# Order of the expert pieces and form of the bias products in a hybrid layer's expert stage

## The chip, the cores and the metric

The kernel runs on one core of a Trainium2 chip. The metric is the device time of one execution in microseconds; lower is better. A profile of one execution shows what each engine did: TensorE (PE, its weight loads apart as PEld), VectorE (DVE), ScalarE (ACT), GpSimd (POOL) and SyncE (SP), which here issues most of the DMAs.

## What is computed

One decoder layer on 1024 tokens of width 1024: attention and convolution, then a mixture of 32 experts with the top 4 for each token, then a per-layer embedding. The change is in the experts:

```python
def expert_rows(args):
    rows, e = args
    gu = rows @ w_gate_up[e] + b_gate_up[e]
    gate = jnp.minimum(gu[:, :D_FF], SWIGLU_LIMIT)
    up = jnp.clip(gu[:, D_FF:], -SWIGLU_LIMIT, SWIGLU_LIMIT)
    hid = (up + 1.0) * (gate * jax.nn.sigmoid(gate * SWIGLU_ALPHA))
    return hid @ w_down[e] + b_down[e]
```

`w_gate_up[e]` is 1024 x 2048 and `w_down[e]` 1024 x 1024, both float32: 12 MB of weights an expert.

## The kernel before

The expert stage goes through a table of items. An item is up to 128 rows of one expert; where an expert has 129 to 160 rows, its item also takes the up to 32 rows above 128 as a tail. The loop of items is the same on every engine, each with its own program and semaphores.

**Pieces.** An item's weights come as 12 pieces of 1 MB, each 128 partitions x 2048 floats. `raw` holds 6 of them. Pieces 0 to 3 hold the first half (512) of the gate columns and the first half of the up columns, 256 rows of the matrix a piece; pieces 4 to 7 the second halves; pieces 8 to 11 are `w_down`. SP issues the loads (`expert_piece`, L492): two DMAs for a piece of gate and up, with rows of 2 KB, one DMA for a piece of down, with rows of 4 KB. A slot of `raw` is free when VectorE has split its piece and a tail has read it, if there is one.

**Splits.** To keep float32's precision, each piece is split in two parts of a faster type (float32r): ScalarE copies `raw` to `whi` (6 slots, L1753), and VectorE writes `wlo` = `raw` - `whi` (4 slots, L876). The activations are split in the same way (`xhi`, `xlo`, `hhi`, `hlo`). TensorE then runs three matmuls for each product (`three`, L608): 12 matmuls of 128 x 512 a piece, 144 an item. Each piece that TensorE has done raises `w_free`, and the splits of later pieces wait for that.

**Activation.** After piece 3 (half 0) and piece 7 (half 1) VectorE clamps `gat` and `upc` (`gate_part`, L885), ScalarE makes `sig` (L1766), VectorE the product and `hid` (`gated`, L893), TensorE transposes `hid` in four blocks (`turn_hidden`, L592), ScalarE and VectorE split it into `hhi` and `hlo`. The first half's transposes are in the middle of piece 6, the second half's after piece 8, and behind them the eight transposes of the next item's rows (`turn_rows`, L575, L580). Pieces 8 and 9 need half 0 of `hhi` and `hlo`, pieces 10 and 11 half 1.

**Bias.** The bias is added by matmuls of a row of ones with the bias in two parts (`bias_pair`, L600, L604): two matmuls over two partitions each, one at partitions 0 and 1, the other at 32 and 33, one for each PSUM bank; three pairs an item, in pieces 0, 4 and 8.

**Tail.** Two pieces at a time, between the other pieces, TensorE multiplies the tail's rows with the unsplit `raw` (`tail_piece`, L653, lines L671 and L679) and adds nothing there; VectorE adds the bias. The tail's activation also runs in two halves (`tail_first`, `tail_gated`, `turn_tail_hidden`). The tail's pieces 0 to 3 run at the end of the item ahead.

The order of the work on each engine is written out by hand in `body(n, k1, tail)`, a loop over the 12 pieces c. What stands at c on VectorE and ScalarE runs in that order, with waits on semaphores; nothing is reordered. `items.ahead` reads the next item's registers.

Before the stage, all engines raise `stage3_end` and wait for all four; ScalarE's part is L1803.

Of the kernel before, what the change touches and what calls it, by code (L numbers as in the profile page):

```python
# [18 lines left out]
P = 128  # L19
F32 = mybir.dt.float32  # L20
F32R = mybir.dt.float32r
# [69 lines left out]
def layer(nc, x, p_in, positions, g_mix_pre, w_in, w_dw, b_dw, g_conv_ln, b_conv_ln, w_out, g_mix_post,  # L91
# [3 lines left out]
    with outer:  # L95
# [129 lines left out]
        sums = sb("sums", [P, 256])  # L225
        gat = sb("gat", [P, 512])
        upc = sb("upc", [P, 512])
        sig = sb("sig", [P, 512])
# [6 lines left out]
        bias_t = sb("bias_t", [P, 2, 2, P])  # L235
# [9 lines left out]
        gat_t = sb("gat_t", [P, P])  # L245
        upc_t = sb("upc_t", [P, P])
        sig_t = sb("sig_t", [P, P])
        hid_t = sb("hid_t", [P, P])
# [106 lines left out]
        gate_done = sem("gate_done")  # L355
# [154 lines left out]
        def raw_value(n, c):  # L510

            first = 32
            second = 32 if c % RAW < 2 else 16
            return n * (first + second) + (first if c < RAW else first + second)
# [43 lines left out]
        def gate_base(half):  # L558
            return 0 if half else 2
# [13 lines left out]
        def experts_pe(pe):  # L573
# [39 lines left out]

            def gate_piece(n, c, turns):
                half, p = c // 4, c % 4
                base = gate_base(half)
                if c == 0:
                    pe.wait_ge(xlo_ready, n + 1)
                    pe.wait_ge(y_used[0], n)
                if c == 4:  # L620
                    pe.wait_ge(gu_used, 2 * n)
                for g in range(2):
                    if c == 6 and g == 1:
                        turns()
                    if p == 0 and g == 1:
                        if half == 0:
                            pe.wait_ge(bias_in[0], 32 * n + 32)
                            pe.wait_ge(y_used[1], n)
                        mm = bias_pair(base, half, True)
                        if half == 1:  # L630
                            mm.then_inc(bias_used[0], 1)
                    for k in range(2):
                        mm = three(banks(base + g), xhi, xlo, 2 * p + k, c, 2 * k + g,
                                   p == 0 and g == 0 and k == 0, p == 3 and k == 1)
                    if p == 3 and g == 0:
                        mm.then_inc(gate_done, 1)
                return mm

            def down_piece(n, c):
                r = c - 8  # L640
                pe.wait_ge(hlo_ready, 2 * n + r // 2 + 1)
                if r == 0:
                    pe.wait_ge(bias_in[1], 32 * n + 32)
                    pe.wait_ge(gu_used, 2 * n + 1)
                    bias_pair(2, 2, False).then_inc(bias_used[1], 1)
# [7 lines left out]
            def tail_piece(n, k1, c):  # L653
# [10 lines left out]
                if c in (8, 10):  # L664
                    pe.wait_ge(ht_ready, 2 * k1 + c // 2 - 3)
# [1637 lines left out]
```

## Time and profile before

| what | value |
|---|---|
| time, median of 3 runs | 2472.63 us (2472.3 to 2474.09) |
| time of the profiled execution | 2471.6 us |
| span of the profile | 2469.9 us |
| granted TensorE clock, share of full | 0.979 |
| busy: PE, DVE, ACT | 95%, 73%, 57% |
| DMA in the span | 629.50 MB, mean 255 GB/s |
| expert stage | about 740 to 2302 us |

The span runs from the first to the last instruction of the profiled execution. Busy time of PE counts overlapping matmuls once, so a busy PE isn't one at its peak. Start times of neighbouring matmuls tell more than their durations, since matmuls are pipelined.

### The profile page before, as it was taken

To read this page: it belongs to the slowest core of one execution; us is meant where nothing else is said; L and a number is where in the kernel's file an instruction comes from. 1 tells how busy PE (TensorE), PEld (TensorE's weight loads), DVE (VectorE), ACT (ScalarE), POOL (GpSimd) and SP (SyncE) were. 2 spreads that over 40 slices of the span, in tenths; PEclk is the share of its full clock that TensorE was granted. 3 is DMA by queue.
4 is the path that set the end of the run, shared out by engine and by line. 5 is a ranking of instruction groups with operands and counts; after the bars stand their busy time and mean duration, and the time that the engine had idled before them with its cause. 6 is when DMAs were issued, how large, how long until landed. Compare 5 with 4: busy or idle time off the path is not lost.

```text
span 2469.9 us, 39207 instructions
## 1 busy us (share of the span) xinstructions
PE 2341.7 (95%) x11242; PEld 1577.9 (64%) x11243; DVE 1807.0 (73%) x2101; ACT 1402.9 (57%) x1441; POOL 257.3 (10%) x252
## 2 busy tenths in 40 slices
PE   6999999999948999999999999999999999999898
PEld 3454445545536777677777777777776777776443
DVE  4582555544557889788989988898877787897374
ACT  2112354434435777667777777677766676776344
POOL 1200000001230000100000001000111010010230
PEclk9999999999959999999999999999999999999999
DMA  6006910052238999999999999899988898997761
GB/s 198 22 13 216 355 36 22 14 185 77 69 96 287 333 352 354 336 311 362 345 375 351 360 365 348 307 338 375 351 287 312 278 360 292 367 347 260 267 221 51
DMA packets 291338, 629.50 MB, mean 255 GB/s; under 512 B 21633, under 2 KB 69505, under 8 KB 291218
## 3 DMA queue, kind: packets, MB, share of 16 engines
q1 hardware_dynamic: 235538, 532.20, 61.4%
q10 hardware_dynamic: 40304, 55.05, 6.2%
q0 software_dynamic: 15440, 41.51, 5.2%
q8 instruction: 33, 0.54, 0.1%
q14 instruction: 23, 0.19, 0.0%
HBM read 558.55 MB, written 68.57 MB: 254 GB/s over the span
## 4 chain that ended last, share of the span: by engine, by line
PE 75%; DVE 12%; issue 5%; DMA 5%; ACT 2%; DVEq 1%; SPq 1%; POOL 0%; ACTq 0%; POOLq 0%
PE bank L610 13%; PE bank L612 12%; PE bank L611 12%; PE bank L1368 6%; DVE wlo L876 6%; PE bank L780 4%; PE bank L1481 4%; PE bank L1391 3%; PE bank L671 3%; DMA raw<-in_w_down_dram 3%; PE bank L1358 2%; PE bank L1411 2%; PE bank L1440 2%; PE bank L1426 2%; PE bank L580 2%
## 5 line engine op out<-in xcount | busy, mean ns | idle before, releaser
L876 DVE TENSOR_TENSOR wlo<-raw,whi 128x2048 fp32r<-128x2048 f32 x456 | 1038.1, 2287 | 203.2 <-PE bank L612 159.8
L1753 ACT ACTIVATE whi<-raw 128x2048 fp32r<-128x2048 f32 x456 | 872.4, 1915 | 351.0 <-PE bank L612 172.8
L610 PE MATMUL bank<-whi,xhi 128*128 128x512 f32 x1216 | 498.3, 410 | 4.2 <-issue 4.2
L612 PE MATMUL bank<-wlo,xhi 128*128 128x512 f32 x1216 | 481.4, 396 | 0.0
L611 PE MATMUL bank<-whi,xlo 128*128 128x512 f32 x1216 | 481.0, 396 | 0.0
L610 PEld LDWEIGHTS bank<-whi,xhi 128*128 128x128 f32 x1216 | 228.7, 188 | 93.3 <-issue 43.4
L612 PEld LDWEIGHTS bank<-wlo,xhi 128*128 128x128 f32 x1216 | 228.8, 188 | 55.0
L611 PEld LDWEIGHTS bank<-whi,xlo 128*128 128x128 f32 x1216 | 229.1, 188 | 47.0
L610 PE MATMUL bank<-whi,hhi 128*128 128x512 f32 x608 | 246.0, 405 | 0.0
L612 PE MATMUL bank<-wlo,hhi 128*128 128x512 f32 x608 | 237.6, 391 | 0.0
L611 PE MATMUL bank<-whi,hlo 128*128 128x512 f32 x608 | 236.9, 390 | 0.0
L1295 POOL DMA_DIRECT2D ids<-token_list x37 | 20.6, 557 | 1117.4 <-PE bank L580 1067.3
L610 PEld LDWEIGHTS bank<-whi,hhi 128*128 128x128 f32 x608 | 114.1, 188 | 33.1 <-issue 12.2
L612 PEld LDWEIGHTS bank<-wlo,hhi 128*128 128x128 f32 x608 | 114.1, 188 | 25.3
L1974 DVE CUSTOM_DVE_ANT_0 S<-bank,mlog 128x512 f32<-128x512 f32 (+3 forms) x144 | 73.1, 554 | 76.5 <-PE bank L1411 53.2
L611 PEld LDWEIGHTS bank<-whi,hlo 128*128 128x128 f32 x608 | 114.4, 188 | 21.5
L1657 ACT ACTIVATE PT<-bank 128x512 f32<-128x512 f32 (+3 forms) x96 | 44.5, 513 | 131.8 <-PE bank L1426 131.8
L780 PE MATMUL bank<-raw,h2T 128*128 128x512 f32 x256 | 111.3, 593 | 1.2 <-ACT h2T L827 1.2
L1481 PE MATMUL bank<-uT,xall 128*128 128x512 f32 x224 | 101.7, 598 | 0.7 <-ACT qT L1698 0.7
L1368 PE MATMUL bank<-uT,wk 128*128 128x512 f32 x192 | 98.5, 634 | 1.2 <-ACT qraw L1632 1.2
L1368 PE MATMUL bank<-uT,wq 128*128 128x512 f32 x192 | 92.6, 610 | 0.1
L1766 ACT ACTIVATE sig<-gat 128x512 f32<-128x512 f32 x76 | 47.3, 623 | 68.9 <-DVE gat L889 68.8
(294 smaller groups left out, 2767.3 us busy)
## 6 DMA issues: line engine op xcount, KB each, us to landing
raw<-in_w_gate_up_dram SPq DMA_DIRECT2D x608, 512.0 KB, 6.5
raw<-in_w_down_dram SPq DMA_DIRECT2D x152, 1024.0 KB, 10.5
expert_rows<-zeros ACTq DMA_DIRECT2D x1, 33280.0 KB, 105.5
expert_rows<-ysb ACTq DMA_DIRECT2D x38, 512.0 KB, 8.1
xall<-in_x_dram SPq DMA_DIRECT2D x8, 512.0 KB, 11.0
uT<-in_w_out_dram SPq DMA_DIRECT2D x1, 4096.0 KB, 12.8
raw<-in_w_ple_gate_dram SPq DMA_DIRECT2D x1, 4096.0 KB, 19.8
h<-h_scratch SPq DMA_DIRECT2D x8, 512.0 KB, 6.2
```

Source lines behind the costliest of these rows:

```text
L580: mm = pe.transpose(banks(XT, 2)[:, k * P:k * P + P], xg[:, k * P:k * P + P], ident)
L610: pe.matmul(dst, stat_hi[:, kt], hi, start=first, stop=False)
L611: pe.matmul(dst, stat_lo[:, kt], hi, start=False, stop=False)
L612: return pe.matmul(dst, stat_hi[:, kt], lo, start=False, stop=last)
L671: mm = pe.matmul(banks(SUM if half else ACC)[j * TAIL:j * TAIL + TAIL, 0:256] .rearrange("m (g n) -> m g n", g=2), xt[:, 2 * p + k], piece ...
L780: mm = pe.matmul(banks(4 + 2 * (t % 2) + half), h2T[t % 2][:, k], wpg[:, k, half * 512:half * 512 + 512], start=(k == 0), stop=(k == KD - 1))
L876: dve.tensor_tensor(wlo[:, c % LO], raw[:, c % RAW], whi[:, c % HI].bitcast(F32), ALU.subtract).then_inc(lo_ready, 1)
L1368: mm = pe.matmul(banks(bank_no), w[:, k], uT[:, k, half * 512:half * 512 + 512], start=(k == 0), stop=(k == KD - 1))
L1391: mm = pe.matmul(banks(b + c)[:, 0:n], uT[:, k, t * P:t * P + P], wv[:, k, c * 512:c * 512 + n], start=(k == 0), stop=(k == KD - 1))
L1481: pe.matmul(banks(2 + half), mixT[:, k, t * P:t * P + P], wout[:, k, half * 512:half * 512 + 512], start=(k == 0), stop=False)
L1753: act.activation(whi[:, c % HI], raw[:, c % RAW], ACT.Copy).then_inc(hi_ready, 1)
L1974: dve.tensor_tensor_reduce(out=S[b][:, c * 512:c * 512 + w], in0=score_bank(s, c, h)[:, 0:w], in1=mlog[:, T - n + c * 512:T - n + c * 512 ...
```

## The change

Pieces 0 to 3 now hold all 1024 gate columns, pieces 4 to 7 all up columns, each loaded by one DMA with rows of 4 KB. The gate's clamp, sigmoid and product are done once, 1024 wide, after piece 3; the up half and `hid` stay in two halves of 512. TensorE runs the first halves of pieces 6 and 7, raises `up_done`, then the second half of piece 6, the transposes of `hid`'s half 0, and the second half of piece 7; the row transposes of the next item come behind piece 7. VectorE's splits from piece 9 on stand one place later. A bias product is one matmul over 128 partitions, where `bsp` has the two bias rows and 126 zero rows; ScalarE writes the zeros once, before the stage. The tail follows the same order: gate, then up, one turn of its hidden rows.

```diff
-        sums = sb("sums", [P, 256])
-        gat = sb("gat", [P, 512])
+        gat = sb("gat", [P, D])
...
-        bsp = sb("bsp", [P, 3, 512], F32R)
+        bsp = sb("bsp", [P, 3 * D], F32R)
...
-                half, p = c // 4, c % 4
-                rows = w_gate_up[0, bass.ds(e, 1), p * 256:p * 256 + 256, :].rearrange(
+                g, p = c // 4, c % 4
+                rows = w_gate_up[0, bass.ds(e, 1), p * 256:p * 256 + 256, g * DFF:g * DFF + DFF].rearrange(
                     "e (k p) n -> p (e k) n", p=P)
-                parts = dst.rearrange("p (k g) n -> p g k n", g=2)
-                for g in range(2):
-                    sp.dma_start(parts[:, g], rows[:, :, g * DFF + half * 512:g * DFF + half * 512 + 512]
-                                 ).then_inc(raw_in[slot], 16)
+                sp.dma_start(dst.rearrange("p (k d) n -> p k (d n)", k=2), rows).then_inc(raw_in[slot], 16)
...
-            def bias_pair(base, block, started):
-
-                for d in range(2):
-                    r = slice(TAIL * d, TAIL * d + 2)
-                    mm = pe.matmul(banks(base + d), one_r[r, :], bsp[r, block, :], start=not (started and d == 0),
-                                   stop=False)
-                return mm
+            def bias_row(dst, block, first):
+
+                return pe.matmul(dst, one_r[:], bsp[:, block * 512:block * 512 + 512], start=first, stop=False)
...
+            def gate_part(n, c, half):
+                g, p = c // 4, c % 4
+                base = gate_base(g)
+                if p == 0 and half == 0:
+                    if g == 0:
+                        pe.wait_ge(xlo_ready, n + 1)
+                        pe.wait_ge(y_used[0], n)
+                    else:
+                        pe.wait_ge(gu_used, 2 * n)
+                if p == 0:
+                    if half == 0 and g == 0:
+                        pe.wait_ge(bias_in[0], 16 * n + 16)
+                    if half == 1 and g == 0:
+                        pe.wait_ge(y_used[1], n)
+                    mm = bias_row(banks(base + half), 2 * g + half, True)
+                    if half == 1 and g == 1:
+                        mm.then_inc(bias_used[0], 1)
+                for k in range(2):
+                    mm = three(banks(base + half), xhi, xlo, 2 * p + k, c, 2 * k + half,
+                               False, p == 3 and k == 1)
+                return mm
+
             def gate_piece(n, c, turns):
...
+                if c == 6:
+                    gate_part(n, 6, 0)
+                    pe.wait_ge(lo_ready, PIECES * n + 8)
+                    gate_part(n, 7, 0).then_inc(up_done, 1)
+                if c == 7:
+                    turns()
+                if c < 6:
+                    gate_part(n, c, 0)
+                return gate_part(n, c, 1)
...
-                    if tail and c == 1:
-                        turn_tail_hidden(k1, 0)
+                    if tail and c == 4:
+                        turn_tail_hidden(k1)
...
-                    if c == 8:
+                    if c == 7:
                         if tail:
-                            hold(pe, ht_ready, 2 * k1 + 2)
+                            hold(pe, ht_ready, k1 + 1)
                         with pe.If(nxt2 > 0):
                             hold(pe, xt_ready, nk1 + 1)
                         with pe.If(nxt > 0):
...
+            def gate_clamp(n):
+
+                dve.wait_ge(w_free, PIECES * n + 4)
+                dve.wait_ge(hid_ready, 2 * n)
+                dve.wait_ge(gs_done, n)
+                dve.tensor_scalar(gat[:], banks(gate_base(0), 2), LIMIT, None, ALU.min).then_inc(gat_ready, 1)
+
+            def gate_product(n):
+
+                dve.wait_ge(sig_done, n + 1)
+                dve.tensor_tensor(sig[:], gat[:], sig[:], ALU.mult).then_inc(gs_done, 1)
+
+            def up_half(n, half):
+
+                if half == 0:
+                    dve.wait_ge(up_done, n + 1)
+                else:
+                    dve.wait_ge(w_free, PIECES * n + 8)
                 dve.wait_ge(hid_ready, 2 * n + half)
...
                 for c in range(PIECES):
-                    if tail and c == 8:
-                        tail_rows(k1, items.kf)
-                    if tail and c == 5:
-                        tail_gated(k1, 1)
-                    if c in (3, 7):
-                        gate_part(n, c // 4)
-                    if c in (5, 7):
-                        gated(n, c // 7)
-                    if c == 8:
-                        hidden(n, 1)
+                    if c == 3:
+                        gate_clamp(n)
+                    if tail and c == 4:
+                        tail_up(k1)
+                        tail_gated(k1)
+                    if c == 4:
+                        gate_product(n)
                     if c == 5:
                         items.ahead(n + 1)
                         nxt, nxt2 = items.value(LIVE), items.value(TWO)
-                    if c + LO < PIECES:
+                    if c in (6, 7):
+                        up_half(n, c - 6)
+                    if tail and c == 8:
+                        tail_rows(k1, items.kf)
+                    if c == 8:
+                        hidden(n, 1)
+                    if c < 5:
                         dve.wait_ge(w_free, PIECES * n + c + 1)
                         split_lo(n, c + LO)
-                    else:
+                    if c in (6, 7, 8):
+                        dve.wait_ge(w_free, PIECES * n + c)
+                        split_lo(n, c + LO - 1)
+                    if c == 6:
+                        hidden(n, 0)
+                    if c >= 9:
                         with dve.If(nxt > 0):
                             if c == 9:
                                 columns(n + 1)
-                            dve.wait_ge(w_free, PIECES * n + c + 1)
-                            split_lo(n + 1, c + LO - PIECES)
-                    if c == 5:
-                        hidden(n, 0)
...
+                            dve.wait_ge(w_free, PIECES * n + c)
+                            split_lo(n + 1, c + LO - PIECES - 1)
+                            if c == 11:
+                                dve.wait_ge(w_free, PIECES * n + PIECES)
+                                split_lo(n + 1, LO - 1)
...
+            hold(sp, ytail_out, rows_stored)
             load5(0)
...
+            for s in range(2):
+                act.wait_ge(u2_out[s], 16 * NT // 2)
+            act.activation(bsp[:].rearrange("p (a n) -> p a n", n=P), ones[:].unsqueeze(1).to_broadcast([P, 3 * KD, P]),
+                           ACT.Copy, scale=0.0).then_inc(bias_zero, 1)
             act.activation(mark3, ident[:, 0:1], ACT.Copy).then_inc(stage3_end, 1)
...
-                    if c == 7:
-                        sigmoid(n, 1)
...
                     if c in (6, 8):
                         hidden(n, c // 8)
...
                     if c == 3:
-                        sigmoid(n, 0)
+                        sigmoid(n)
```

ScalarE's `split_hi(n, c + 6)` stands at c ahead of the sigmoid at c = 3, as before; its `columns` of the next item's rows stand at c = 7 instead of 8.

## Rows read from the trace of the kernel before

**Rows 1.** The page: busy time of the engines in the span.

```profile
PE 2341.7 (95%) x11242; PEld 1577.9 (64%) x11243; DVE 1807.0 (73%) x2101; ACT 1402.9 (57%) x1441; POOL 257.3 (10%) x252
```

**Rows 2.** Groups of instructions, 740 to 2300: count, busy us, mean ns, idle before.

```profile
L604 PE MATMUL bank<-bsp,one_r 2*128 2x512 f32 x228 | 57.0, 496 | 1.4 <-issue 1.4
...
L1766 ACT ACTIVATE sig<-gat 128x512 f32<-128x512 f32 x76 | 47.3, 623 | 68.9 <-DVE gat L889 68.8
L881 DVE TENSOR_TENSOR xlo<-bank,xhi 128x1024 fp32r<-128x1024 f32 x37 | 45.0, 1216 | 0.0
```

**Rows 3.** Waits of PE, 740 to 2300: us in total, times, longest.

```profile
PE bank L597 <- DVE hid L901: 20.9, 31, 1.4
PE bank L687 <- DVE hid_t L930: 6.0, 8, 2.9
```

**Rows 4.** Timeline of ACT: start, us; an item's last row, twice.

```profile
1230.69 0.60 ACT L1786 ACTIVATE ysb<-bank 128x512 f32<-128x512 f32 x1 [0.24 <-PE bank L612]
...
1268.69 0.60 ACT L1786 ACTIVATE ysb<-bank 128x512 f32<-128x512 f32 x1 [0.24 <-PE bank L612]
```

**Rows 5.** Timeline of PE around a bias pair.

```profile
1231.84 0.40 PE L612 MATMUL bank<-wlo,xhi 128*128 128x512 f32 x1
1232.16 0.50 PE L604 MATMUL bank<-bsp,one_r 2*128 2x512 f32 x2
1232.59 0.49 PE L610 MATMUL bank<-whi,xhi 128*128 128x512 f32 x1
1232.93 0.39 PE L611 MATMUL bank<-whi,xlo 128*128 128x512 f32 x1
1233.15 0.40 PE L612 MATMUL bank<-wlo,xhi 128*128 128x512 f32 x1
```

**Rows 6.** Timeline of all engines at the end of piece 8.

```profile
1257.90 0.39 PE L612 MATMUL bank<-wlo,hhi 128*128 128x512 f32 x1
1258.02 0.69 DVE L901 SCALAR_TENSOR_TENSOR hid<-upc,sig 128x512 f32<-128x512 f32 x1
...
1258.77 0.65 PE L597 MATMUL bank<-cst,hid 128*128 128x128 f32 x4 [0.48 <-DVE hid L901]
1259.37 1.06 PE L580 MATMUL bank<-cst,xg 128*128 128x128 f32 x8
...
1260.19 0.48 PE L610 MATMUL bank<-whi,hhi 128*128 128x512 f32 x1
1260.51 0.40 PE L611 MATMUL bank<-whi,hlo 128*128 128x512 f32 x1
```

**Rows 7.** Timelines of SP, ACT, POOL and DVE in that item.

```profile
1233.82 0.37 SPq L507 DMA_DIRECT2D raw<-in_w_down_dram  x1
...
1244.89 1.92 ACT L1753 ACTIVATE whi<-raw 128x2048 fp32r<-128x2048 f32 x1 [0.70 <-DMA raw<-in_w_down_dram]
1246.71 0.61 ACT L1766 ACTIVATE sig<-gat 128x512 f32<-128x512 f32 x1
...
1266.06 1.85 POOL L1297 DMA_INDIRECT xg<-u_scratch,ids  x1 [4.41 <-DMA ids<-token_list]
...
1264.77 6.68 DVE L876 TENSOR_TENSOR wlo<-raw,whi 128x2048 fp32r<-128x2048 f32 x3
```

**Rows 8.** Windows with down pieces, then gate and up pieces; last: clock, DMA share, GB/s.

```profile
1241.00:1247.00 6.00, 6.00 (x27) 4.44 (x26) 5.47 (x5) 4.89 (x4) 0.00 (x0) 1.00 1.03 415
1250.00:1256.00 6.00, 6.00 (x29) 4.50 (x28) 5.10 (x4) 4.32 (x3) 0.00 (x0) 1.00 1.05 387
```

**Rows 9.** Timeline at the stage's start, and a later tail at full clock.

```profile
730.72 0.19 ACT L1803 ACTIVATE conv<-cst 128x1 f32<-128x1 f32 x1
...
750.65 0.45 PE L687 MATMUL bank<-cst,hid_t 128*128 128x128 f32 x1 [2.93 <-DVE hid_t L930]
751.02 3.27 PE L671 MATMUL bank<-raw,xt 128*32 128x256 f32 x32
...
1039.40 1.93 PE L671 MATMUL bank<-raw,xt 128*32 128x256 f32 x32
```

More of the change, by code:

```diff
@@ L224, in layer @@
         ysb = sb("ysb", [P, D])
[L225 to L226 removed]
+        gat = sb("gat", [P, D])
         upc = sb("upc", [P, 512])
[L228 removed]
+        sig = sb("sig", [P, D])
         hid = sb("hid", [P, 512])
@@ L354, in layer @@
         w_free = sem("w_free")
-        gate_done = sem("gate_done")
+        up_done = sem("up_done")
         table_set = sem("table_set")
@@ L510, in raw_value @@
         def raw_value(n, c):
-            first = 32
-            second = 32 if c % RAW < 2 else 16
-            return n * (first + second) + (first if c < RAW else first + second)
+            return 32 * n + 16 * (c // RAW + 1)
         class Items:
@@ L556, in run, with gate_base @@
                                     body(n, k1, False)
-        def gate_base(half):
-            return 0 if half else 2
+        def gate_base(g):
+            return 0 if g else 2
         XT, SUM, HT, ACC = 4, 5, 6, 7
@@ L612, in three @@
                 return pe.matmul(dst, stat_hi[:, kt], lo, start=False, stop=last)
-            def gate_piece(n, c, turns):
[L615 to L637, printed above, removed]
@@ L682, in tail_piece, with turn_tail_hidden @@
                 mm.then_inc(tail_free, 1)
-            def turn_tail_hidden(k1, half):
-                hold(pe, hid_t_ready, 2 * k1 + half + 1)
-                hold(pe, ht_ready, 2 * k1 + half)
-                pe.transpose(banks(XT)[:, 0:P], hid_t[:], ident).then_inc(htt_done, 1)
+            def turn_tail_hidden(k1):
+                hold(pe, hid_t_ready, k1 + 1)
+                hold(pe, ht_ready, k1)
+                for s in range(2):
+                    mm = pe.transpose(banks(XT)[:, s * P:s * P + P], hid_t[:, s * P:s * P + P], ident)
+                mm.then_inc(htt_done, 1)
             turn_rows(0)
@@ L706, in turns @@
                     if tail:
-                        turn_tail_hidden(k1, 1)
                         pe.wait_ge(sums_ready, 2 * k1 + 2)
@@ L1762, in tail_columns, with sigmoid @@
                                ACT.Copy).then_inc(xt_ready, 1)
-            def sigmoid(n, half):
-                act.wait_ge(gat_ready, 2 * n + half + 1)
+            def sigmoid(n):
+                act.wait_ge(gat_ready, n + 1)
                 act.activation(sig[:], gat[:], ACT.Sigmoid, scale=ALPHA).then_inc(sig_done, 1)
@@ L1813, in body @@
                 for c in range(PIECES):
-                    if tail and c == 2:
-                        tail_hidden(k1, 0)
-                    if c == 7:
-                        with act.If(nxt2 > 0):
-                            tail_columns(nk1)
+                    if tail and c == 5:
+                        tail_hidden(k1)
                     if c == 0:
@@ L1821, in body @@
                         act.activation(mark[:], ident[:, 0:1], ACT.Sigmoid).then_inc(table_set, 1)
-                    if c == 7:
-                        sigmoid(n, 1)
-                    if tail and c == 5:
-                        tail_sigmoid(k1, 1)
                     if c in (6, 8):
                         hidden(n, c // 8)
-                    if tail and c == 6:
-                        tail_hidden(k1, 1)
+                    if c == 6:
+                        with act.If(nxt2 > 0):
+                            tail_columns(nk1)
                     if c == 11:
@@ L1834, in body @@
                         split_hi(n, c + HI)
+                    elif c == 7:
+                        with act.If(nxt > 0):
+                            act.wait_ge(w_free, PIECES * n + c + 1)
+                            split_hi(n + 1, c + HI - PIECES)
+                            columns(n + 1)
                     else:
```

125 lines of the change are left out of this document (58 added, 67 removed).

## The prediction

> **What bounds the kernel now.** I read the page's line of busy time first: TensorE 95%, VectorE 73% [rows 1]. The reader is to see that only TensorE has no room. Next the groups of instructions from 740 to 2300 us, the expert stage: L604, a bias matmul, stands there 228 times, six to an item, so there are 38 items [rows 2]. Then the waits of TensorE in that stage: on `hid` 31 times for 20.9 us, on `hid_t` 8 times for 6.0 us, almost nothing on weights [rows 3]. So the weights arrive in time as things stand, eight items have a tail, and the stage's length is the sum of what TensorE runs, plus short waits for its own activation. Last the timeline. Two neighbouring items end 38.00 us apart (1230.69 to 1268.69) [rows 4]. That is the period of an item without a tail, and I work out what it is made of.
>
> Matmuls of the stage start 0.233 us apart (1232.93 to 1233.15 is 0.22, most are 0.23) [rows 5]. An item has 12 x 12 = 144 of them: 33.55 us. A bias pair: the matmul before it starts at 1231.84, the one after the next at 1232.93, 1.09 us, where two steps of 0.233 would be 0.47 [rows 5]. A pair thus costs 0.62 us, three of them 1.87. Transposes cost by the same reading: eight take 1.06 of which the last alone is 0.30, so they start 0.109 apart, and after them a matmul follows almost at once but the next only 0.32 later (1260.19 to 1260.51) [rows 6]; n of them between matmuls cost 0.11 + 0.109 (n - 1): four cost 0.44, twelve 1.31. At the end of piece 8 the last matmul starts at 1257.90, and the transpose of `hid` only at 1258.77, when `hid` is done: 0.87 instead of 0.23, a wait of 0.64 [rows 6]. Sum: 33.55 + 1.87 + 0.44 + 1.31 + 0.64 + some 0.18 at the item's border = 38.0. It closes, so each term may be changed by itself.
>
> **Bias products.** Six pairs' members become six full matmuls in the stream: 6 x 0.233 = 1.40 for 1.87, saving 0.47 us an item. The trace has no full matmul with the bias, but L610 is the same kind and size and stands next to it [rows 5]. Bounds: nothing saved beyond the second instruction, if the gaps stay with the bias (cost 3 x 0.233 = +0.70), and -0.47. I take -0.47: the gaps are on both sides of L604 (0.32 in, 0.43 and 0.33 out), and the full matmul is the same form as what surrounds it. The Trainium skill ("TensorE: Matmul & The Clock Gate", Part 3, Packing small matmuls) says that matmuls of small K in different row groups run at once; by it a pair costs one matmul, and the change costs 3 x 0.233 = 0.70 us an item instead of saving. The two do start together here (x2 at 1232.16) [rows 5], so that much agrees. "TensorEngine Tiling", Key Properties, adds that changing the tiling mode drains the engine; the gaps of rows 5 look like that.
>
> **Transposes and waits.** The eight row transposes move from behind the second hidden group to the end of piece 7, the hidden groups keep four each: 0.44 + 0.87 + 0.44 = 1.75, as before (0.44 + 1.31). The wait of 0.64 goes: after piece 7 VectorE needs `upc` and `hid`, some 0.7 each, and TensorE has 0.87 of transposes and 3.26 of piece 8. So the fixed part becomes 33.55 + 1.40 + 1.75 + 0.18 = 36.88, 1.12 less.
>
> Three new waits stand against it. First: `up_half(0)` starts when the first halves of pieces 6 and 7 are done. A matmul lasts 0.39 from its start (1257.90 [rows 6]), with the hand-over 0.42; upc and hid take 0.69 each as hid does there, with gaps 1.40: 1.87 with the hand-over back, and TensorE has only six matmuls meanwhile, 1.63. Wait 0.24, and 0.06 in its transposes: 0.30. Second: piece 8 wants `hlo`, which VectorE writes after the split of piece 9: hid ends at T+1.82 (T: start of the last matmul ahead of `up_done`), split until T+4.03, hlo until T+4.7; TensorE is there at T+4.5. Wait 0.25. Third: the gate product on VectorE (now 1024 wide, as L881: 1.22 [rows 2]) stands in front of the split of piece 8 and needs the sigmoid, which ScalarE puts behind its split of piece 9. T is at 20.4 from the item's start (88 matmuls of 0.233). Backward: VectorE must be free at 20.8; splits follow each other in 2.2 (three in 6.68 [rows 7]), product 1.22, so the product starts by 17.4; the sigmoid is now some 1.05 with hand-over, the copy in front of it 1.82 (1244.89 to 1246.71 [rows 7]); piece 9 must have landed by 14.5. What is late beyond that costs TensorE the same.
>
> When does it land? Now its load is issued at 1233.82, 3.2 after the item's start (0.1 ahead of `ysb`'s 1230.69 [rows 4]), and the copy starts at 1244.89, waiting for the DMA: 11.1 after issue, 14.3 after the start [rows 7]. There `sig` had slack, since `gated` stood behind the split of piece 8; here it hasn't. And the new order has VectorE split pieces 0 and 1 of the next item one place later: walking it with 2.2 for a split, `hlo` of half 1 at T+9.5 and xlo 1.22, the slot of piece 3 is free at 5.35, issue 5.7, which is 2.5 later than now. By the same 11.1 it would land at 16.8. But the backlog is smaller: the gather of `xg`, now issued at 1266.06, 2.5 ahead of the item's end, so that it moves in just this stretch [rows 7], goes out some four us earlier with the row transposes; and rows of 4 KB move at 415 GB/s where those of 2 KB move at 387, both with the DMA share above 1.0 [rows 8]. Six, seven, `ysb`, eight and nine are 4.5 MB from 1.1 on, at 0.40 MB/us 11.3 us, with some 2 for the store and the last engine: 14.5. I take a wait of 0.3. Ends: 0 and 2.35.
>
> Regular item: -1.12 + 0.30 + 0.25 + 0.30 = -0.27 us; 30 of them, -8.1 us. ScalarE and VectorE also save fixed parts of ops (sig 2 x 0.62 [rows 2] to about 1.03), and SP one issue of two; these lie in slack and count only through the third wait.
>
> **Tail items.** Six groups of tail matmuls stay. `turn_tail_hidden` is once for twice, later, when `hid_t` is ready: the 6.0 us of waits over eight [rows 3] go, of which the first, 2.93, is in the start below; the rest is 0.44 each. One transposing fewer is about 0.26 (0.32 for leaving one [rows 6], less the second column's 0.06 of new work, an estimate): -0.70 each. Bias -0.47, first wait +0.30; the old 0.64 isn't there with a tail behind piece 7, nor the new second. Sum -0.87, times 8: -7.0 us.
>
> **Start.** ScalarE zeroes 128 x 3072 of `bsp` ahead of its mark for stage 3's end. The mark is at 730.72 [rows 9]; I take it as the last to come, so this delays everything. Between 512 wide 0.623 [rows 2] and 2048 wide 1.92 [rows 7] lies 0.84 ns an element, 2.8 us for 3072. Against it the first tail item's stall goes: 2.93 us idle, and 32 tail instructions at 3.27 where the same take 1.93 at full clock [rows 9], 1.34; the stall drops it to the lower level. Net -1.5. At the end SP waits for stores that are long done: nothing; they have piece 9 to 11 as cover.
>
> **Sum.** -8.1 - 7.0 - 1.5 = -16.6. The profiled execution took 2471.6 (span 2469.9), so 2455.0; the median is 1.0 above it: 2456. A measurement tells 0.2%, 5 us.
>
> **Rivals.** Covered: the DMA is early and hlo too (both waits at 0), -0.82 a regular item: -24.6 - 8.5 = -33, 2440. For it: faster rows [rows 8], and each load is one DMA where there were two. Against: hlo is behind a split by program order.
>
> Eaten up: piece 9 lands 0.9 late: -1.12 + 0.55 + 0.9 = +0.33, 30 times +10, minus 8.5: 2474, no change. The gain turns over to loss at 0.85 us late (landing 15.4), tails and start counted.
>
> Late piece, the one on the other side: the load keeps its 11.1 us, lands at 16.8, 2.35 late, +1.78 an item, +53 - 8.5: 2517; halfway 2495. One mechanism: the sigmoid behind the copy of piece 9 holds `gate_product`, split 8 and `up_half`. For it: ScalarE's copy of piece 9 waits for the DMA now, 0.70 us [rows 7]. Against: less backlog, faster rows.
>
> Pairs were cheap: gaps stay, bias +0.70 instead of -0.47, 38 x 1.17 = +44: 2500. Against it: rows 5.
>
> **Chances and range.** Forecast (2446 to 2466) 0.42, covered 0.17, eaten up 0.13, late 0.23, pairs 0.05. Faster: 0.42 + 0.17 + 0.05 of the third = 0.64; same: the third's other 0.08 and 0.03 of the late one = 0.11; slower: 0.20 + 0.05 = 0.25. The range leaves out the best of the covered case and the far part of the late one, 0.06 and 0.14: 2434 to 2492.
>
> **What the profile after would show.** Full bias matmuls 0.23 from their neighbours, 228 of them (else pairs were cheap). TensorE idle ahead of the `hid` transposes of half 0 by 0.2 to 0.3, none at half 1. A wait of piece 8's first bias product for hlo. ScalarE's copy ahead of the sigmoid at 14 to 15 from the item's start, and `sig` product by 17.4; if later, `hid` waits of over 0.5 per item and a period above 38. Regular period 37.7. `hid_t` waits gone. Mark 2.8 later. It would be wrong if VectorE, with 12 x 2.28 + 3 x 1.22 + 6 x 0.69 = 35 us of work in 37.7 and idle twice by order, slips behind and weights are waited for on TensorE.

## The result, and the profile after

| kernel | median, us | lowest to highest | runs |
|---|---|---|---|
| before | 2472.47 | 2470.52 to 2474.09 | 4 |
| after | 2504.25 | 2501.48 to 2510.22 | 4 |

The ratio is 1.0131, interval 1.0119 to 1.0143: the changed kernel is slower by 1.3%, 31.8 us. The forecast was 2456 in a range of 2434 to 2492. It had the wrong sign and the range doesn't hold the time.

The page of the kernel after, busy time:

```profile
PE 2338.4 (93%) x11242; PEld 1614.1 (64%) x11243; DVE 1787.6 (71%) x1993; ACT 1397.4 (56%) x1388; POOL 246.2 (10%) x252
```

TensorE's busy time is 3 us less than in [rows 1] and the span 34.2 us more (2504.1 for 2469.9). The work shrank and the idle time grew. Who is waited for, over the expert stage (740 to 2340 us), with total, times and longest:

```profile
PE bank L591 <- DVE hid L911: 45.5, 28, 4.6
PE bank L600 <- issue: 10.8, 8, 1.4
```

The transposes of `hid` were waited for 31 times for 20.9 us before [rows 3]. Now it is 28 times for 45.5, and one such wait takes up to 4.6. The waits for `hid_t` are gone, but eight of 1.4 us, with no releaser but the issue itself, stand in their place.

**Where the 34.2 us are.** An item ends with its second `ysb` row on ScalarE, as in [rows 4]. Means over the distances of these rows, from the whole stage's timeline of ScalarE:

| items | count | before, us each | after, us each | difference in all, us |
|---|---|---|---|---|
| up to the first item's end | 1 | 791.4 | 785.4 | -6.0 |
| second item | 1 | 43.3 | 44.6 | +1.3 |
| plain: no tail in it or behind it | 23 | 38.10 | 38.11 | +0.2 |
| ahead of a tail (it runs the tail's first pieces) | 6 | 42.05 | 47.03 | +29.9 |
| with a tail | 7 | 48.30 | 49.53 | +8.6 |
| after the last item's end | | 168.5 | 168.8 | +0.3 |

The reader is to see that 23 items came out even and six paid 5 us each. A mean over the 38 items would have hidden both.

**A plain item.** Timeline of TensorE, one that starts at 1191.4: the end of the six matmuls ahead of `hid`, and the row transposes.

```profile
1213.51 0.40 PE L602 MATMUL bank<-wlo,xhi 128*128 128x512 f32 x1
1214.54 0.66 PE L591 MATMUL bank<-cst,hid 128*128 128x128 f32 x4 [0.64 <-DVE hid L911]
...
1216.43 1.03 PE L574 MATMUL bank<-cst,xg 128*128 128x128 f32 x8
1217.39 0.47 PE L596 MATMUL bank<-bsp,one_r 128*128 128x512 f32 x1
```

From the last matmul to the transpose it is 1.03 here, 1.25 on average over the 23 plain items (0.50 to 1.76), where 0.23 is no wait. The second half's gap is 0.23 in all items: the wait of 0.64 [rows 6] has gone. Behind the row transposes, piece 8's bias product follows at once (0.96 after they begin), so there is no wait for `hlo`. What `hid` waits for stands on ScalarE, in the same item:

```profile
1204.28 1.92 ACT L1771 ACTIVATE whi<-raw 128x2048 fp32r<-128x2048 f32 x1 [0.66 <-DMA raw<-in_w_down_dram]
1206.84 1.92 ACT L1771 ACTIVATE whi<-raw 128x2048 fp32r<-128x2048 f32 x1 [0.64 <-DMA raw<-in_w_down_dram]
1208.66 1.04 ACT L1784 ACTIVATE sig<-gat 128x1024 f32<-128x1024 f32 x1
```

and on VectorE:

```profile
1203.85 1.23 DVE L892 TENSOR_SCALAR gat<-bank 128x1024 f32<-128x1024 f32 x1 [0.43 <-PE bank L602]
...
1209.73 1.23 DVE L897 TENSOR_TENSOR sig<-gat,sig 128x1024 f32<-128x1024 f32 x1 [2.46 <-ACT sig L1784]
1210.88 2.29 DVE L878 TENSOR_TENSOR wlo<-raw,whi 128x2048 fp32r<-128x2048 f32 x1
1213.08 0.68 DVE L906 TENSOR_SCALAR upc<-bank 128x512 f32<-128x512 f32 x1
1213.80 0.69 DVE L911 SCALAR_TENSOR_TENSOR hid<-upc,sig 128x512 f32<-128x512 f32 x1
```

`gat` is ready at 1205.1, but the sigmoid starts at 1208.66, because two copies that wait for the DMA stand ahead of it. VectorE idles 2.46 us, and product, split, `upc` and `hid` follow without a pause: whatever the product is late, `hid` is late too.

**An item ahead of a tail.** Timeline of ScalarE, from the end of one item to the end of the next, 46.47 us:

```profile
981.89 0.60 ACT L1805 ACTIVATE ysb<-bank 128x512 f32<-128x512 f32 x1 [0.23 <-PE bank L602]
...
997.84 1.92 ACT L1771 ACTIVATE whi<-raw 128x2048 fp32r<-128x2048 f32 x1 [3.13 <-DMA raw<-in_w_down_dram]
1000.67 1.92 ACT L1771 ACTIVATE whi<-raw 128x2048 fp32r<-128x2048 f32 x1 [0.92 <-DMA raw<-in_w_down_dram]
1002.49 1.04 ACT L1784 ACTIVATE sig<-gat 128x1024 f32<-128x1024 f32 x1
...
1028.36 0.60 ACT L1805 ACTIVATE ysb<-bank 128x512 f32<-128x512 f32 x1 [0.24 <-PE bank L602]
```

Piece 9's copy starts 18.8 after the item's start (1000.67 from 981.89), not 15.4 (1206.84 from 1191.4). The mean over the six items ahead of a tail is 18.9, over the 23 plain ones 15.4. On TensorE:

```profile
1003.69 0.40 PE L602 MATMUL bank<-wlo,xhi 128*128 128x512 f32 x1
1008.37 1.12 PE L591 MATMUL bank<-cst,hid 128*128 128x128 f32 x4 [4.29 <-DVE hid L911]
...
1011.85 0.63 PE L600 MATMUL bank<-whi,xhi 128*128 128x512 f32 x1
1012.28 0.63 PE L601 MATMUL bank<-whi,xlo 128*128 128x512 f32 x1
```

TensorE starts nothing for 4.68 us. Afterwards its matmuls start 0.43 apart instead of 0.23. The granted clock over 1008 to 1012 is 0.50 (third column from the end), its lower level, 1.2 GHz:

```profile
1008.00:1012.00 4.00, 3.63 (x16) 2.95 (x17) 3.12 (x3) 2.08 (x3) 0.00 (x0) 0.50 0.99 374
```

So the stall costs more than its length: from the transposes of `hid` to those of the next item's rows it takes 4.76 here, and 2.70 in the same item of kernel 8 below, where the clock stays up. In all six such items it takes 4.0 to 4.8. In that item GpSimd fetches for the tail (timeline of POOL):

```profile
985.91 2.00 POOL L1325 DMA_INDIRECT xgt<-u_scratch,ids_t  x1 [5.86 <-issue]
987.90 2.18 POOL L1331 DMA_DIRECT2D bias_t<-in_b_gate_up_dram  x4
990.05 2.01 POOL L1337 DMA_DIRECT2D bias_d<-in_b_down_dram  x4
```

Two stretches of that time, and one of the plain item; the last three columns are granted clock, DMA share and GB/s:

```profile
987.00:992.00 5.00, 5.00 (x23) 4.02 (x22) 5.00 (x4) 3.06 (x3) 5.00 (x9) 1.00 1.03 407
992.00:997.00 5.00, 5.00 (x23) 4.02 (x22) 4.72 (x3) 1.92 (x1) 0.06 (x1) 1.00 1.03 283
...
1197.00:1203.00 6.00, 6.00 (x27) 4.83 (x26) 6.00 (x3) 4.09 (x4) 0.00 (x0) 1.00 1.03 421
```

The DMA engines are full in all three, yet they move 283 GB/s behind the issues of GpSimd and 407 to 421 otherwise. The DMA queues over 15 us of this item (985 to 1000): packets, MB, share of the 16 engines.

```profile
q1 hardware_dynamic: 1046, 4.03, 81.0%
q0 software_dynamic: 304, 0.52, 12.5%
```

and over 15 us at the same place of the plain item (1194.7 to 1209.7):

```profile
q1 hardware_dynamic: 1363, 5.26, 93.4%
```

GpSimd's 0.52 MB take 12.5% of 15 us, 1.9 us of all engines. SP's weights besides move at 4.03 / (0.81 x 15) = 0.33 MB/us for 5.26 / (0.934 x 15) = 0.375. Together the weights get 1.23 MB less, which at 0.375 is 3.3 us; piece 9 is later than in a plain item by 3.4. Experiment 7 tests this.

**An item with a tail.** Timeline of TensorE behind the turn of `hid_t`:

```profile
1049.03 0.40 PE L602 MATMUL bank<-wlo,xhi 128*128 128x512 f32 x1
1049.48 0.41 PE L689 MATMUL bank<-cst,hid_t 128*128 128x128 f32 x2
1051.26 0.49 PE L600 MATMUL bank<-whi,xhi 128*128 128x512 f32 x1 [1.36 <-issue]
```

The program has there `turn_tail_hidden`, which holds TensorE's sequencer until `hid_t` is ready, and right behind it `items.ahead`, which reads the next item's registers. A guess at this point: the reads used to run while matmuls were still queued, and now nothing is queued.

### The profile page after: what moved, and what is told of

It is laid out like the page before. It is cut to its first block, busy times and chain, and to the rows that moved or that the text cites. A ratio compares the mean times of both kernels' runs of the same rounds, so it can differ in the third digit from the quotient of the medians.

```text
span 2504.1 us, 37980 instructions
## 1 busy us (share of the span) xinstructions
PE 2338.4 (93%) x11242; PEld 1614.1 (64%) x11243; DVE 1787.6 (71%) x1993; ACT 1397.4 (56%) x1388; POOL 246.2 (10%) x252
## 4 chain that ended last, share of the span: by engine, by line
PE 56%; DMA 14%; DVE 13%; issue 11%; ACT 3%; DVEq 2%; SPq 1%; ACTq 0%; POOL 0%; POOLq 0%
DMA raw<-in_w_down_dram 11%; DVE wlo L878 7%; PE bank L600 6%; PE bank L1386 6%; PE bank L602 6%; PE bank L601 6%; PE bank L782 4%; PE bank L1499 4%; PE bank L1409 3%; PE bank L673 2%; PE bank L1376 2%; PE bank L1429 2%; PE bank L591 2%; PE bank L1458 2%; PE bank L574 2%
## 5 line engine op out<-in xcount | busy, mean ns | idle before, releaser
L878 DVE TENSOR_TENSOR wlo<-raw,whi 128x2048 fp32r<-128x2048 f32 x456 | 1025.0, 2283 | 41.1 <-PE bank L602 40.3
L600 PE MATMUL bank<-whi,xhi 128*128 128x512 f32 x1216 | 490.8, 404 | 10.8 <-issue 10.8
L1788 ACT ACTIVATE hhi<-bank 128x512 fp32r<-128x512 f32 x76 | 45.6, 600 | 148.9 <-PE bank L591 148.9
L897 DVE TENSOR_TENSOR sig<-gat,sig 128x1024 f32<-128x1024 f32 x38 | 46.5, 1224 | 98.5 <-ACT sig L1784 98.5
L596 PE MATMUL bank<-bsp,one_r 128*128 128x512 f32 x228 | 99.2, 435 | 8.7 <-issue 4.7
```

What stands on the lines that cost most here:

```text
L596: return pe.matmul(dst, one_r[:], bsp[:, block * 512:block * 512 + 512], start=first, stop=False)
L600: pe.matmul(dst, stat_hi[:, kt], hi, start=first, stop=False)
L878: dve.tensor_tensor(wlo[:, c % LO], raw[:, c % RAW], whi[:, c % HI].bitcast(F32), ALU.subtract).then_inc(lo_ready, 1)
```

## The experiments

All are timed against the kernel before on the same chip; its medians were 2471.82 for the first four below, 2469.62 for the next four, 2470.91 for the last three. Beside the run of the kernel after it was 2472.47, so between these groups a difference of medians is good to some 3 us, and the ratios give a second value. "Gap" is the distance from the last matmul to the first transpose of `hid`, half 0, unless the other half is named; 0.23 is no wait.

**1. The sigmoid ahead of the copy of piece 9** (ScalarE, after the change):

```diff
+                    if c == 3:
+                        sigmoid(n)
                     if c + HI < PIECES:
                         act.wait_ge(w_free, PIECES * n + c + 1)
                         split_hi(n, c + HI)
...
-                    if c == 3:
-                        sigmoid(n)
```

> Changed kernel, with ScalarE's sigmoid ahead of its copy of piece 9 instead of behind it. Queue theory (the sigmoid stands behind a copy that waits for a late load, and holds the gate product, the split of piece 8 and the first half of hid): in items without a tail behind them the wait ahead of the transposes of hid, half 0, falls from about 1.25 to 0.51 from matmul to transpose, 23 items by 0.7 = -17 us; in the six items ahead of a tail the sigmoid still stands behind the copy of piece 8, which ended its wait at 16 us of the item: some -3 each, -18; time 2504 - 35 = 2469. Rival, the late weights themselves hold TensorE: no change, 2504. Rival, the bias products or the rows of 4 KB cost it: no change, 2504.

2462.05, ratio 0.9962 (0.9946 to 0.9979); 2469 was expected. One moved line turns a loss of 1.3% into a gain of 0.4%. The waits of TensorE for `hid`:

```profile
PE bank L591 <- DVE hid L911: 8.1, 6, 1.8
```

They are left in six items, those ahead of a tail. Plain items take 37.43 with a gap of 0.51, items ahead of a tail 42.38: 0.68 and 4.65 less than in the changed kernel. The late sigmoid is the cause of the wait in both.

**2. The sigmoid one copy earlier still,** with `c == 2` in the same place, so ahead of the copy of piece 8.

> Changed kernel, with the sigmoid ahead of ScalarE's copy of piece 8. Queue theory: as with the sigmoid ahead of piece 9 in the plain items (-17), and in the six items ahead of a tail the whole wait of 4.2 us goes, and with it the drop of the clock: -28; time 2459. If only piece 9's copy matters: the same as the run with the sigmoid ahead of piece 9. Rivals with weights, bias products or rows as the cause: 2504.

2463.02, ratio 0.9966 (0.9950 to 0.9982): no better than experiment 1, where I had expected 10 us. The gap is 0.51 in every item, so the `hid` wait has gone but for the 0.28 that every item of the new order has. It has a successor, in items ahead of a tail (42.79):

```profile
PE bank L574 <- ACT xt L1779: 11.5, 6, 2.1
```

`xt`, ScalarE's copy of the tail's rows, stands behind copies of late pieces too, and the row transposes of the next item wait for it. With pieces landing this late the wait moved to the next operation in ScalarE's order.

**3. Only VectorE's order:** the gate product behind the split of piece 8.

```diff
-                    if c == 4:
+                    if c == 5:
                         gate_product(n)
```

> Changed kernel, ScalarE as it is, with VectorE's gate product behind the split of piece 8 (where it stood before the change). Queue theory: the split of 2.2 us no longer waits for the sigmoid, so the plain items lose their excess wait (-17); ahead of a tail hid comes 2.1 earlier of 4.2, -13; time 2474. Rivals with the cause elsewhere: 2504.

2473.37, ratio 1.0009 (0.9995 to 1.0024). Plain items take 37.42, as in experiment 1: with one split less between the product and `hid`, the late sigmoid is absorbed. Items ahead of a tail still have gaps of 2.4 to 3.5 and take 44.15.

**4. Register reads first** (TensorE): `items.ahead` ahead of `turn_tail_hidden`.

```diff
+                    if c == 4:
+                        items.ahead(n + 1)
+                        nxt, nxt2 = items.value(LIVE), items.value(TWO)
                     if tail and c == 4:
                         turn_tail_hidden(k1)
...
-                    if c == 4:
-                        items.ahead(n + 1)
-                        nxt, nxt2 = items.value(LIVE), items.value(TWO)
```

> Changed kernel, with TensorE's reading of the next item's registers ahead of the turn of the tail's hidden rows instead of right behind it. Theory: behind the turn, which waits for hid_t in the sequencer, the reads lie open, 1.36 us of idle TensorE in each of 8 tail items: 2504 - 11 = 2493. Rival, the idle time is the change of matmul form or the wait of hid_t itself: 2504.

2492.81, ratio 1.0079 (1.0057 to 1.0101). Timeline of TensorE at the same place:

```profile
1051.70 0.40 PE L602 MATMUL bank<-wlo,xhi 128*128 128x512 f32 x1
1052.18 0.41 PE L689 MATMUL bank<-cst,hid_t 128*128 128x128 f32 x2
1052.35 0.48 PE L600 MATMUL bank<-whi,xhi 128*128 128x512 f32 x1
```

From transposes to matmul it is 0.17 instead of 1.78, and items with a tail take 47.93 instead of 49.53. The others don't move (plain 38.13, ahead 46.98). The guess is confirmed.

**5. The bias products alone:** the kernel before, with one matmul over 128 partitions for each bias product, the zeros and one DMA per load, all else as before.

```diff
...
-                    r = slice(TAIL * d, TAIL * d + 2)
-                    mm = pe.matmul(banks(base + d), one_r[r, :], bsp[r, block, :], start=not (started and d == 0),
-                                   stop=False)
+                    b = 2 * d + block if block < 2 else 4 + d
+                    mm = pe.matmul(banks(base + d), one_r[:], bsp[:, b * 512:b * 512 + 512],
+                                   start=not (started and d == 0), stop=False)
...
```

> Kernel before, with the bias products alone changed: one matmul over 128 rows with zero rows for each bank, the zeros written on ScalarE ahead of the stage. Prediction's step: -0.47 us an item in 38 items, -18, and +2.8 for the zeros: 2457. Rival, pairs were cheap and the gaps stay: +0.70 an item, +27 and +2.8: 2502.

2464.73, ratio 0.9977 (0.9962 to 0.9992): faster, by 5 us where 15 were expected. Timeline of TensorE around two bias products and back:

```profile
1150.66 0.40 PE L612 MATMUL bank<-wlo,xhi 128*128 128x512 f32 x1
1150.89 0.63 PE L604 MATMUL bank<-bsp,one_r 128*128 128x512 f32 x2
1151.36 0.39 PE L610 MATMUL bank<-whi,xhi 128*128 128x512 f32 x1
```

From the matmul before to the one after it is 0.70, three steps of 0.233, for 1.09 in [rows 5]. Most plain items take 37.7, 0.3 less than 38.0 and not 0.47 less, since the gap at `hid` half 1 is now 1.05 for 0.87: what TensorE saves ahead of a wait, it partly waits. The six items ahead of a tail gain nothing in this profile (42.32 for 42.05).

**6. Rows of 2 KB:** the changed kernel with each gate or up piece in two DMAs, half a row each.

```diff
-                sp.dma_start(dst.rearrange("p (k d) n -> p k (d n)", k=2), rows).then_inc(raw_in[slot], 16)
+                parts = dst.rearrange("p (k d) n -> p d k n", d=2)
+                for d in range(2):
+                    sp.dma_start(parts[:, d], rows[:, :, d * 512:d * 512 + 512]).then_inc(raw_in[slot], 16)
...
```

> Changed kernel, with each gate or up piece loaded by two DMAs with rows of 2 KB instead of one with rows of 4 KB. If rows of 4 KB land pieces earlier (415 against 387 GB/s in the windows of before): piece 9, behind three such pieces in the queues, lands some 0.5 later, the sigmoid holds all 29 items without a tail by that: 2504 + 15 = 2519. If one big DMA lands later than two small ones, as the rival has it: faster, 2490. If rows don't matter: 2504.

2516.43, ratio 1.0186 (1.0166 to 1.0206). In plain items piece 9 lands at 15.7 on average for 15.4 (15.1 to 16.3), and they take 38.55, 0.44 more. So rows of 4 KB are worth 12 us to the changed kernel, 14 by the ratios (1.0186 for 1.0131). Two DMAs for one belong to this difference; they weren't told apart.

**7. The tail's bias loads later:** GpSimd holds them until half 0 of `hid` is done in the item that it fetches in, the one ahead of the tail.

```diff
+                    hold(pool, hid_ready, 2 * n - 1)
                     hold(pool, sums_ready, 2 * k)
                     for j in range(GROUPS):
                         pool.dma_start(bias_t[j * TAIL:j * TAIL + TAIL],
```

> Changed kernel, with Pool's loads of the next tail's two biases held back until the item's first half of hid is done, so that they don't meet pieces 8 and 9 in the DMA queues. Theory (small packets of these loads slow pieces 8 and 9 in the six items ahead of a tail, which land at 18.8 instead of 15.4): landing back near 16, the wait there from 4.7 to about 2: -16 and some clock, 2486. Rival, the gather of the tail's rows is what slows them: no change, 2504.

2480.94, ratio 1.0049 (1.0032 to 1.0066). The item starts 2 us later in this profile (983.85), so the stretch of 283 GB/s is now 994 to 999 (same columns):

```profile
994.00:999.00 5.00, 5.00 (x23) 4.04 (x22) 4.74 (x3) 3.42 (x2) 0.00 (x0) 1.00 1.02 360
```

Ahead of a tail, piece 9 lands at 16.2 to 16.5 instead of 18.8, the gap is 2.1 to 2.4 instead of 4.7, and the item takes 42.76 for 47.03. Eight DMAs of 32 and 64 KB were most of the late landing, 2.5 of 3.4 us. The mean of 42.76 again hides two kinds: in three of the six items the matmuls behind the wait start 0.43 apart, at a granted clock of 0.50 to 0.56, and those items take 43.2 to 45.0; in the other three the clock stays at 1.00 and they take 41.7.

**8. Four repairs together:** experiments 2, 3, 4 and 7 in the changed kernel.

> Changed kernel with all four repairs: sigmoid ahead of the copy of piece 8, gate product behind the split of piece 8, registers first, Pool's tail bias loads late. Queue theory: plain items at 37.3, ahead of a tail at 42.3, tail items at 47.9: 2504 - 17 - 28 - 11 = 2448, under both kernels. If the weights are late by themselves once the waits are gone, it stays at 2465 or above.

2434.14, ratio 0.9856 (0.9838 to 0.9874): 1.4% faster than the kernel before, and faster than each experiment so far. 2448 was expected; nearly all of the rest, 13 us, lies in the six items ahead of a tail, expected at 42.3. With the loads of experiment 7 out of the way the wait for `xt` of experiment 2 is gone too. The waits of TensorE in the stage that have to do with an item's activation are gone but for the 0.28; the largest of the items' waits, besides two at the program's issue, is

```profile
PE bank L596 <- ACT ysb L1806: 4.3, 9, 1.0
```

Plain items take 37.40 (37.24 at least), those ahead of a tail 40.09, those with one 47.92. In the item ahead of a tail, ScalarE now does

```profile
991.06 1.07 ACT L1785 ACTIVATE sig<-gat 128x1024 f32<-128x1024 f32 x1 [1.56 <-DVE gat L892]
992.03 3.70 ACT L1772 ACTIVATE whi<-raw 128x2048 fp32r<-128x2048 f32 x2
996.24 1.92 ACT L1772 ACTIVATE whi<-raw 128x2048 fp32r<-128x2048 f32 x1 [0.50 <-DMA raw<-in_w_down_dram]
```

The sigmoid waits for `gat` alone. The item started at 977.4 (its predecessor's end): the sigmoid is at 13.7, where it was at 20.6.

**9. Bias over two partitions,** in kernel 8: a single matmul for each product as in the change, but over the two rows that hold the bias.

```diff
-                return pe.matmul(dst, one_r[:], bsp[:, block * 512:block * 512 + 512], start=first, stop=False)
+                return pe.matmul(dst, one_r[0:2, :], bsp[0:2, block * 512:block * 512 + 512], start=first, stop=False)
```

> The version with the four repairs, with each of its six bias products an item over the two rows that hold the bias instead of over 128 rows with zeros; position and order unchanged. If the gaps beside a bias product come from its form (as beside the pairs in the kernel before: 0.32 in, 0.43 and 0.33 out instead of 0.23 each), each costs 0.62 instead of 0.23, and six by 38 items make 0.39 x 228 = +89: 2434 + 89 = 2523. Rival, only the number of matmuls counts: 2434.

2510.15, ratio 1.0160 (1.0141 to 1.0178), so 76 us above kernel 8. Plain items take 39.31, 1.91 more, and all within 0.05 of each other. Timeline of TensorE:

```profile
1198.46 0.39 PE L602 MATMUL bank<-wlo,hhi 128*128 128x512 f32 x1
1198.88 0.49 PE L596 MATMUL bank<-bsp,one_r 2*128 2x512 f32 x1
1199.30 0.50 PE L600 MATMUL bank<-whi,xhi 128*128 128x512 f32 x1
1199.63 0.39 PE L601 MATMUL bank<-whi,xlo 128*128 128x512 f32 x1
...
1200.57 0.40 PE L602 MATMUL bank<-wlo,xhi 128*128 128x512 f32 x1
1200.89 0.50 PE L596 MATMUL bank<-bsp,one_r 2*128 2x512 f32 x1
```

The second of the two stands in the full stream, as four of the six do: 0.32 in, then 0.43 and 0.33 out (1201.32, 1201.65), just as round the pair of [rows 5]. That is some 1.09 for 0.70 in kernel 8, 0.39 more. So the gaps belong to the change of form, not to there being two. The first (1198.88) opens the item, where kernel 8 has 0.43 to 0.85 ahead of the bias product too (five neighbouring items), and the fifth stands behind the row transposes, where kernel 8 also has a gap; these two cost less, and the mean over an item is 1.91 / 6 = 0.32. The Trainium skill ("TensorEngine Tiling (Array Packing)", Key Properties) says that switching the tiling mode drains the engine. The gaps on both sides agree with that; the trace shows them, not the drain itself.

**10. Rows of 2 KB in kernel 8,** the edit of experiment 6 there, to see whether the row's size still counts once nothing stands behind a late piece.

> The version with the four repairs, with gate and up pieces loaded by two DMAs each with rows of 2 KB. Queue theory: landings 0.3 later as in the run with rows of 2 KB on the changed kernel, but nothing waits for them any more: 2434, at most +3. Rival, row size counts by itself: +12 as there, 2446.

2442.55, ratio 0.9880 (0.9856 to 0.9904): 8 us above kernel 8, 6 by the ratios, between the two numbers expected. There is again no wait for `hid`, but

```profile
PE bank L600 <- ACT ysb L1810: 11.9, 16, 1.7
```

Sixteen items' first bias products wait 11.9 us for ScalarE's `ysb`, nine for 4.3 in kernel 8. `ysb` too stands behind a copy that waits for the DMA, that of one of the next item's gate and up pieces (L1776 at 1214.04 waits 0.92 us for its piece, `ysb` follows at 1215.87). The same fault as the sigmoid's, at another place.

**11. The late bias loads in the kernel before,** the edit of experiment 7 there.

> Kernel before, with Pool's loads of the next tail's biases held back until the first half of hid. If these loads slow the pieces there as well, the six items ahead of a tail go from 42.1 to near 40.5: -10, 2461. Rival, only the changed order was exposed to them: 2471.

2458.26, ratio 0.9950 (0.9930 to 0.9970). The waits for `hid` are 13.5 us for the 20.9 of [rows 3], items ahead of a tail take 40.42 for 42.05. These loads cost the kernel before as well; there they cost 12 us, in the changed one 23 (2504.25 to 2480.94), or 20 by the ratios (1.0131 to 1.0049).

## Why the prediction was wrong

**Wrong: the third wait, in its size and above all in its count.** The prediction put 0.3 on the sigmoid that stands behind ScalarE's copy of piece 9, and multiplied by 30 items alike. The mechanism is the one that decides (experiments 1 and 3), and the issue, forecast at 5.7, came at 5.8 (SP issued piece 9 at 1197.18 in the item that starts at 1191.4). Two things failed.

First, the landing in plain items was worked out as 14.5 and is 15.4, from the sum of 4.5 MB at 0.40 MB/us with 2 us for the store (1.1 + 11.3 + 2, which is 14.4). The product starts at 18.3 instead of 17.4, and 0.74 us of wait come of it (gap 1.25 less 0.51) instead of 0.3. The plain item is -1.12 + 0.28 + 0.74 = -0.10 by the forecast's own terms, measured 0.01. That is nearly the point named under "eaten up", where the sum is nothing.

Second, six of the thirty items aren't plain. In them GpSimd's loads for the next tail share the engines, piece 9 lands at 18.8, the gap is 4.7, TensorE loses 4.5 us and then its clock level, which costs another 1.3 to 2.1 (4.01 to 4.76 from the transposes of `hid` to the row transposes, for 2.70 in kernel 8). Experiment 7 shows that these loads are the cause of 2.5 of the 3.4 us by which it is late; the other 0.9 is open. Against that stand the old `hid` wait of such an item, about 1.5 (gaps 1.66 to 1.82 in four of them), and the bias's 0.47; measured is a loss of 29.9 us over the six. The "late piece" rival had the right mechanism and sign, but one price for all items: 1.78 for 30. Measured are 0 for 23 and 5.0 for 6. The rows to see this were in the trace of before: the period of these items, 42.05, wasn't read, and GpSimd's queue was looked at for the gather alone.

**Wrong: items with a tail,** -0.87 forecast, +1.23 measured. The waits for `hid_t` did go. The step that failed is "`turn_tail_hidden` is once for twice, later, when `hid_t` is ready": it overlooked `items.ahead` behind it. That costs 1.60 (experiment 4: 49.53 to 47.93). Without it the tail items are at -0.37, so another 0.5 of the forecast isn't there; 0.17 of it is the bias, which brought 0.30 in these items too (experiment 5: 48.00 for 48.30). The remaining 0.3 is open.

**Right: the bias products,** each 0.233 in the stream, six for 1.40 instead of 1.87. Experiments 5 and 9 settle the "pairs were cheap" rival: leaving the 128-row form for one matmul costs 0.39 in the full stream, 0.32 on average. The Trainium skill ("TensorE: Matmul & The Clock Gate", Part 3, Packing small matmuls) says that matmuls of small K in different row groups run at once. By that the full form would have cost 0.70 more an item (3 x 0.233); experiment 5 gained 0.30. Members of a pair do start together, but the way in and out costs more than the second member saves.

**Right: the first wait,** 0.30 forecast, 0.28 where nothing else is late (gap 0.51 less 0.23, experiments 1, 2 and 8). **Right: the old wait of 0.64 goes.** **Too large: the second wait,** 0.25 for `hlo` ahead of piece 8; no such wait shows. With it at 0 the plain item's floor is 36.88 + 0.28 = 37.16, and kernel 8 has 37.24.

**The start, nearly.** The zeros take 2.75 us ahead of the mark:

```profile
724.57 2.75 ACT L1824 ACTIVATE bsp<-ones 128x3072 fp32r<-128x3072 f32 x1
727.23 0.19 ACT L1826 ACTIVATE conv<-cst 128x1 f32<-128x1 f32 x1
```

2.8 were forecast. From the mark to the first item's end it is 58.1 us for 60.7: -2.6 where -4.27 was forecast, so the start brings nothing instead of -1.5. All that lies ahead of the zeros came 6 us earlier in this profile (`xhi` at 721.85 for 728.00). The profiles of the thirteen kernels here put that `xhi` anywhere from 720.4 to 728.0 and the first item's end from 783.6 to 791.4; among the ten that come from the changed kernel alone `xhi` varies from 720.4 to 725.6. So most of the 6 can be a difference between executions; that none of it comes from the change isn't shown. The forecast also took the first tail item's wait twice, 2.93 in the start and 0.44 in eight times -0.87.

**The sum,** then: forecast -16.6, from -8.1 (30 items), -7.0 (tails), -1.5 (start). Measured in the stage +1.3 + 0.2 + 29.9 + 8.6 = +40, less 6 ahead of it. The second item's 1.3 us is no more than what profiles of one kernel order differ by here (43.2 to 44.8 in the changed one's). Open stays how the DMA engines share their time between the queues: that small loads slow the large ones is shown by the queue rows and by experiment 7, the reason isn't.

## What to carry to other kernels

On an engine that works in order, a small operation that others wait for must not stand behind one that waits for a DMA: the sigmoid, `xt` and `ysb` each paid for it in turn, and moving a handful of lines turned +1.3% into -1.4%. Before a price is multiplied by a count, sort the periods of the loop: items with other traffic or other work in them are another case, and a margin that holds in 23 items can break in six. What a sequencer does right behind a semaphore wait can lie open, as the reading of registers did here for 1.6 us an item; ahead of the wait it cost nothing.

## What the runs showed of the hardware

- A matmul over 2 partitions in the full stream of matmuls over 128 cost 0.39 us more than the same matmul over 128 partitions with 126 zero rows (1.09 for 0.70 over three steps), 0.32 on average over an item's six (39.31 for 37.40). Zero rows were cheaper than leaving them out.
- 0.52 MB of GpSimd's loads took 1.9 us of all 16 DMA engines, 3.6 us a MB (0.125 x 15 / 0.52), where the weights took 2.7 a MB in a plain item (0.934 x 15 / 5.26) and 3.0 beside those loads.
- Rows of 2 KB for rows of 4 KB, with two DMAs for one, cost 12 us over the 304 gate and up loads in the changed kernel (14 by the ratios), and 8 (6 by the ratios) where nothing waited for the sigmoid.
- Reading an item's registers behind a semaphore wait cost TensorE 1.6 us; ahead of it, nothing.
- After an idle time of 4.3 us TensorE's granted clock was 0.50 over 1008 to 1012; behind the wait of 0.64 of the plain item above it stayed at its upper level (matmuls 0.24 apart from 1215.27 on). Between them the length of the wait alone didn't decide: of the twelve waits of 1.4 to 2.1 us ahead of a tail in experiments 2 and 7, five were followed by 0.50 to 0.56 and seven by 1.00, and in experiment 7 one of 1.75 by 0.56, another of 1.75 by 1.00.
